# Inverting the mixer's triangular matrices on one side only, with 32x32 transposes on VectorE, in a hybrid RWKV-7 / gMLP / cross-attention / SwiGLU block

## The reference, cut to what matters

```
def step(S, inp):                 # one token, all heads
    r_t, w_t, k_t, v_t, kk_t, a_t = inp
    sa = jnp.einsum('bhvk,bhk->bhv', S, -kk_t)
    S = (S * w_t[:, :, None, :]
         + sa[..., None] * (kk_t * a_t)[:, :, None, :]
         + v_t[..., None] * k_t[:, :, None, :])
    y = jnp.einsum('bhvk,bhk->bhv', S, r_t)
    return S, y
```

## Time and profile before

| | |
|---|---|
| median of 3 runs | 3065.03 us (3062.26 to 3070.91) |
| span of the profiled execution, first to last instruction | 3061.7 us |
| PE, busy | 2955.4 us, 97% |
| DVE, busy | 1613.3 us, 53% |
| POOL, busy | 1432.3 us, 47% |
| ACT, busy | 1001.8 us, 33% |

### The profile page before, as it was taken

The page is one execution under the profiler, slowest core; times in us unless marked ns, Lnnn a source line. Parts: engine busy times, 40 slices in busy tenths (PEclk is TensorE's granted clock), DMA queues, the critical chain, the costliest instruction groups (busy, mean ns, idle before and its releaser), DMA issues.

```text
span 3061.7 us, 62501 instructions
## 1 busy us (share of the span) xinstructions
PE 2955.4 (97%) x26858; PEld 2523.8 (82%) x26858; DVE 1613.3 (53%) x2010; ACT 1001.8 (33%) x1692; POOL 1432.3 (47%) x993
## 2 busy tenths in 40 slices
PE   8999999989998989999999999999999999999998
PEld 7888888788888878998788888787898788888887
DVE  6332643365666653234866664545232876665452
ACT  4123211233443442233433332222232433332222
POOL 4555454333443445437544442446625654443344
PEclk9999999988998999999999999999999999999999
DMA  4433454321112222111223326454111123335642
GB/s 167 165 102 111 159 161 157 123 59 43 43 49 67 68 60 93 42 42 42 110 110 138 138 111 254 173 198 158 42 48 49 69 110 125 138 125 217 231 152 85
DMA packets 176012, 347.25 MB, mean 113 GB/s; under 512 B 47232, under 2 KB 104576, under 8 KB 170112
## 3 DMA queue, kind: packets, MB, share of 16 engines
q1 hardware_dynamic: 175744, 343.35, 32.5%
HBM read 240.53 MB, written 102.76 MB: 112 GB/s over the span
## 4 chain that ended last, share of the span: by engine, by line
PE 70%; DVE 6%; issue 2%; DMA 2%; ACT 1%; POOL 1%; SPq 0%; DVEq 0%; ACTq 0%; POOLq 0%
PE ps L2201 28%; PE ps L1641 19%; PE ps L2153 6%; PE ps L1747 2%; PE ps L1911 2%; PE ps L1913 2%; PE ps L1895 2%; PE ps L1865 1%; DMA w_raw<-in_weights 1%; DVE tu L2481 1%; DMA hidden<-hid 1%; PE ps L1992 1%; PE ps L1796 1%; PE ps L1819 1%; PE ps L1851 1%
## 5 line engine op out<-in xcount | busy, mean ns | idle before, releaser
L803 POOL TENSOR_TENSOR w_lo<-w_raw,w_hi 128x512 fp32r<-128x512 f32 x256 | 383.1, 1519 | 503.8 <-ACT w_hi L1093 500.0
L1641 PE MATMUL ps<-a_hi,w_hi 128*128 128x512 f32 x1140 | 446.3, 391 | 16.1 <-DVE a_lo L2381 9.6
L1641 PE MATMUL ps<-a_lo,w_hi 128*128 128x512 f32 x1140 | 444.4, 390 | 0.0
L1093 ACT ACTIVATE w_hi<-w_raw 128x512 fp32r<-128x512 f32 x252 | 144.8, 623 | 656.9 <-PE ps L1641 509.8
L1641 PE MATMUL ps<-a_hi,w_lo 128*128 128x512 f32 x1140 | 351.5, 390 | 0.0
L2201 PE MATMUL ps<-a_hi,w_hi 128*128 128x512 f32 x800 | 314.8, 393 | 10.3 <-ACT u_t L1462 4.9
L2201 PE MATMUL ps<-a_lo,w_hi 128*128 128x512 f32 x800 | 313.2, 391 | 0.0
L2201 PE MATMUL ps<-a_hi,w_lo 128*128 128x512 f32 x800 | 312.9, 391 | 0.0
L1641 PEld LDWEIGHTS ps<-a_hi,w_hi 128*128 128x128 f32 x1140 | 214.5, 188 | 62.9 <-DVE a_lo L2381 9.6
L1641 PEld LDWEIGHTS ps<-a_hi,w_lo 128*128 128x128 f32 x1140 | 214.3, 188 | 44.9
L1641 PEld LDWEIGHTS ps<-a_lo,w_hi 128*128 128x128 f32 x1140 | 214.5, 188 | 44.1 <-issue 0.2
(11 more groups left out here) (369 smaller groups left out, 6658.3 us busy)
## 6 DMA issues: line engine op xcount, KB each, us to landing
w_raw<-in_weights SPq DMA_DIRECT2D x228, 512.0 KB, 4.0
hidden<-hid SPq DMA_DIRECT2D x44, 1024.0 KB, 3.9
zT<-z_out SPq DMA_DIRECT2D x44, 512.0 KB, 3.8
a_hi<-hidden SPq DMA_DIRECT2D x44, 512.0 KB, 8.2
a_lo<-hidden SPq DMA_DIRECT2D x44, 512.0 KB, 9.1
w_raw<-kvw SPq DMA_DIRECT2D x32, 512.0 KB, 3.2
suv<-zT SPq DMA_DIRECT2D x16, 512.0 KB, 5.0
x<-in_xT SPq DMA_DIRECT2D x16, 512.0 KB, 6.1
```

The source lines that it names most:

```text
L803: pool.tensor_tensor(low_t[:, u, part, :], w_raw[:, u, part, :], high[:, u, part, :].bitcast(F32), ALU.subtract).then_inc(S["w_lo_done"], 1)
L1093: act.activation(split_into(pair)[0][:, u, part, :], w_raw[:, u, part, :], ACT.Copy).then_inc(S["w_hi_done"], 1)
L1641: mm = pe.matmul(to[:, nb, 0:w], wt[:, u, k, :], r[:, k, nb * w:(nb + 1) * w], start=(k == 0 and r is hi_in and wt is w_hi), stop=(k == kn ...
```

## The change

T is no longer computed on PE. The tile `tu`, which held T and U, becomes `inv`, which holds U alone, and `inv_t`, which holds T. DVE makes `inv_t` from `inv` by its 32x32 block transpose, two instructions a level (`turned`). The entries beside the diagonal are now copied with a mask straight from the scores in PSUM, so `first_pairs` and its semaphore are gone. T, U, `xm` and the right-hand sides all lie on the chunk's own lane a, so `up` is gone. Last, `body` is written in another order on PE and DVE; on ACT the order stays, and only `identities` gets half as long; on POOL nothing changes.

```diff
-            def up(e, a):
-                return a ^ 1 ^ e
+        def new_bank(lv, g):
+            return 2 * g + 1 if lv else 1 - g
...
             def cross(n, par, lv):
                 b = LEVELS[lv]
+                if lv == 0:
+                    pe.wait_ge(S["ev_b"], 2 * n + 2)
                 for g in range(2):
-                    pe.wait_ge(S["tu_ev"], 12 * n + 2 * lv + (g + 1 if lv else 2))
-                    for mh, e, a, h in by_tile(g):
-                        t_u = tu[par][lane(a), g, 0, e, mh, :].rearrange("p (n two b) -> p n two b", two=2, b=b)[:, :, 0, :]
-                        mm = pe.matmul(unit(h, 2 * g * (lv > 0) + e, 2 * L + g * C * (lv == 0) + mh * 32, 32),
-                                       atrb[par][lane(a), e, 2 * mh + g, 0, :], t_u, start=True, stop=True)
+                    if lv == 1 and g:
+                        pe.wait_ge(S["ev_k"], 2 * n + 2)
+                    pe.wait_ge(S["inv_tr"], 10 * n + 2 * lv + g + 1)
+                    for mh, e, a in by_tile():
+                        t_u = inv_t[lane(a), g, 2 * e + mh, :].rearrange("p (n two b) -> p n two b", two=2, b=b)[:, :, 0, :]
+                        mm = pe.matmul(unit(a, 2 * g * (lv > 0) + e, 2 * L + g * C * (lv == 0) + mh * 32, 32), atrb[par][lane(a), e, 2 * mh + g, 0, :], t_u,
+                                       start=True, stop=True)
                     mm.then_inc(S["x_ps"], 1)
...
             def merge(n, par, lv):
...
-                        if not last:
-                            t_at = (2 * g + 1, mh * 32) if e else (2 * g, BANK - C + mh * 32)
-                            pe.matmul(unit(a, *t_at, 32), u_u,
-                                      x_u.rearrange("p (n two b) -> p n two b", two=2, b=b)[:, :, 0, :], start=True, stop=True)
-                        mm = pe.matmul(unit(h, 2 * g + 1, (e + 1) * C + mh * 32, 32), x_u,
-                                       u_u.rearrange("p (n two b) -> p n two b", two=2, b=b)[:, :, 1, :], start=True, stop=True)
+                        mm = pe.matmul(unit(a, new_bank(lv, g), (e + 1) * C + mh * 32, 32), xm[lane(a), e, g, mh, :], u_u, start=True, stop=True)
...
             def from_values(k, par):
-                        mm = pe.matmul(unit(up(e, a), 4 + e, j * L + (m % 2) * C), qkrm[par][lane(a), e, m, 0, :], v_tok[par][lane(a), m, e, :],
+                        mm = pe.matmul(unit(a, 4 + e, j * L + (m % 2) * C), qkrm[par][lane(a), e, m, 0, :], v_tok[par][lane(a), m, e, :],
...
             def solve(k, par, j, last=False):
-                    mm = pe.matmul(unit(a, 6 + e, (2 + j) * L + (m % 2) * C), tu[par][lane(up(e, a)), m % 2, 1, e, m // 2, :],
-                                   rhs_t[lane(up(e, a)), e, m % 2, :], start=False, stop=True, skip_group_check=True)
+                    mm = pe.matmul(unit(a, 6 + e, (2 + j) * L + (m % 2) * C), inv[par][lane(a), e, m, :],
+                                   rhs_t[lane(a), e, m % 2, :], start=False, stop=True, skip_group_check=True)
...
+            def turned(n, par, lv):
+                for g in range(2):
+                    dve.wait_ge(S["tu_ev"], 11 * n + (2 * lv + g if lv else 1))
+                    dve.transpose(inv_t[:, g], units(inv[par], g)).then_inc(S["inv_tr"], 1)
...
             def take_level(n, par, lv):
                 b = LEVELS[lv]
                 for g in range(2):
                     dve.wait_ge(S["tu_ps"], 10 * n + 2 * lv + g + 1)
...
+                    take(rights(inv[par], g, b), low[:, lv + 1, 1].rearrange("p (m n b) -> p m n b", m=HP, b=b),
+                         ps[:, new_bank(lv, g), C:3 * C].rearrange("p (m n b) -> p m n b", m=HP, b=b), "tu_ev")
+                if lv + 1 < len(LEVELS):
+                    turned(n, par, lv + 1)
```

More of the change, by code:

```diff
@@ L238, in hybrid_block_kernel @@
         qkrm = [rw(f"qkrm{i}", [P, 2, HP, 2, C]) for i in range(2)]
-        tu = [rw(f"tu{i}", [P, 2, 2, 2, 2, C]) for i in range(2)]
+        inv = [rw(f"inv{i}", [P, 2, HP, C]) for i in range(2)]
+        inv_t = rw("inv_t", [P, 2, HP, C])
         gate = [tile4(f"gate{i}") for i in range(2)]
@@ L1867, in scores, with by_tile @@
                 mm.then_inc(S[done], 1)
[L1869 to L1886, removed]
+            def by_tile():
+                return [(mh, e, a) for mh in range(2) for e in range(2) for a in range(2)]
@@ L1901, in merge @@
                 b = LEVELS[lv]
[L1902 removed]
                 for g in range(2):
                     pe.wait_ge(S["x_ev"], 10 * n + 2 * lv + g + 1)
[L1905 to L1908, removed]
[L1909 to L1914 removed]
+                    for mh, e, a in by_tile():
+                        u_u = inv[par][lane(a), e, 2 * mh + g, :].rearrange("p (n two b) -> p n two b", two=2, b=b)[:, :, 1, :]
+                        mm = pe.matmul(unit(a, new_bank(lv, g), (e + 1) * C + mh * 32, 32), xm[lane(a), e, g, mh, :], u_u, start=True, stop=True)
                     mm.then_inc(S["tu_ps"], 1)
@@ L1958, in state_in @@
                 for m, e, a in by_pair(j):
[L1959 removed]
+                    mm = pe.matmul(unit(a, 4 + e, j * L + (m % 2) * C), qr[par][lane(e), 0, m, a, :], h_st[lane(e), j, m, :],
                                    start=False, stop=True, skip_group_check=True)
@@ L2009, in body @@
                     state_add(k, par, 0)
+                if behind:
+                    cross(b, q, 0)
+                if state:
                     chunk_out(k, par, 0)
-                if behind:
-                    first_pairs(b, q)
-                if state:
                     state_out(k, par, 1)
@@ L2016, in body @@
                 if behind:
-                    cross(b, q, 0)
+                    merge(b, q, 0)
                 if state:
@@ L2020, in body @@
                 if behind:
-                    merge(b, q, 0)
+                    cross(b, q, 1)
                 if state:
@@ L2024, in body @@
                 if behind:
-                    cross(b, q, 1)
+                    merge(b, q, 1)
                 if state:
@@ L2030, in body @@
                 if behind:
-                    merge(b, q, 1)
+                    cross(b, q, 2)
                 if ahead:
@@ L2035, in body @@
                     variance(k)
+                if behind:
+                    merge(b, q, 2)
                 if ahead:
@@ L2038, in body @@
                 if behind:
-                    cross(b, q, 2)
                     turn(b, kt, "kt_done", 4, ahead, "ktr")
-                    merge(b, q, 2)
+                    cross(b, q, 3)
                     turn(b, bt, "bt_done", 5, ahead, "btr")
-                    cross(b, q, 3)
+                    merge(b, q, 3)
                     turn_v(b, q, ahead, state)
-                    merge(b, q, 3)
+                    cross(b, q, 4)
                     bonus_sums(b, q)
@@ L2048, in body @@
                     key_scales(n)
+                if behind:
+                    merge(b, q, 4)
                 if state:
@@ L2488, in take_scores @@
                     take(dst[:, e].rearrange("p m w t -> p (m w t)"), triangles, ps[:, bank + e, :], done)
-            def blocks(ap, b):
-                return ap.rearrange("p u (n b) -> p u n b", b=b)
+            def turned(n, par, lv):
+                for g in range(2):
+                    dve.wait_ge(S["tu_ev"], 11 * n + (2 * lv + g if lv else 1))
+                    dve.transpose(inv_t[:, g], units(inv[par], g)).then_inc(S["inv_tr"], 1)
             def take_first(n, par):
-                dve.wait_ge(S["sc_1"], n + 1)
+                dve.wait_ge(S["sc_b"], n + 1)
                 dve.wait_ge(S["id_done"], n + 1)
[L2496 to L2500, removed]
+                odd_cols = inv[par][:].rearrange("p e m (x two) -> p e m x two", two=2)[:, :, :, :, 1]
+                mask = low[:, 0, 1].rearrange("p (m x) -> p m x", m=HP).unsqueeze(1).to_broadcast([P, 2, HP, C // 2])
+                take(odd_cols, mask, ps[:, 0:2, :].rearrange("p e (m w x two) -> p e m w x two", w=2, x=C // 2, two=2)[:, :, :, 0, :, 1], "tu_ev")
+                turned(n, par, 0)
             def take_level(n, par, lv):
@@ L2652, in body @@
                     keys_normed(n, state)
+                if scores:
+                    take_level(b, q, 4)
                 if state:
@@ L2657, in body @@
                     mixed(n)
-                if scores:
-                    take_level(b, q, 4)
-                if ahead:
                     decayed(n)
```

40 lines of the change are left out of this document (18 added, 22 removed).

## The result

The changed kernel takes 3101.49 us (median of 4 runs, 3089.15 to 3103.31) against 3064.24 us of the kernel before on the same chip (3062.26 to 3070.91): 1.0096 of it, 95% interval 1.0063 to 1.0129. It is slower, where 3049 us was forecast, and lies outside the range of 3029 to 3082 us. The profiled execution was its fastest, 3089.15 us at a mean clock of 0.977; the other three had 0.969 to 0.970. The ratios in this document leave out two slow runs, one of 3679.58 us at a mean clock of 0.746 in experiment 9 and one of 3074.43 us at 0.976 in experiment 6.

The account below looks back on a forecast made before the run. Took PE to bound the second part, code and DVE waits to slow the first. First part -1.5, second +1.0 us, times 16 = -8; clock -8; 3061.7 - 16 = 3045.7, plus 3.3: 3049 us; range 3029 to 3082 us.

Parts of the forecast that it names:

- the clock: Mixer bodies: the lower clock costs about 21 us before the change; 8 us of it credited as gain.
- the waits for code: First part of a body, PE's "issue" stretches: from 3.1 to 1.0 us, -2.1 us a body.
- Rival 2: The clock falls in the second part instead, 7 us at 1.2 GHz in two bodies of three, 21 us: 3064 us; chance 0.19.
- the end of the second part: After `merge` 4, half the scales (0.55) and 2.1 us for `lora_g` and `mix_gate`: ends at L + 18.3, L being the start of `loras`.
- terms for the second part at full clock: PE waits of 1.7 us at `merge` 3, 0.6 at `cross` 4, 0.3 at `merge` 4; the part +1.0 us.
- The transposes: DVE's block transposes, a price without a row: 0.37 us net each, about six of ten on the path.
- rival 3: The transpose on DVE is dear, 0.8 us each, adding 41 us: 3090 us; chance 0.10.
- A `cross` on two quarters: PE, each `cross` on two quarters of the array: from 0.60 to 1.0 us.
- The first part: Body from `from_values` to `loras`: from 14.5 us in the mean to 13.0 us, -1.5 us a body.
- `cross` 0 waits: First part, PE at `cross` 0: a new wait of 0.75 us for DVE's copies of the scores.
- rival 4: First part's code waits stay 3.1 us because they follow the transfers, +34 us: 3083 us; chance 0.13.
- Rival 1: Code waits vanish and the clock stays full, 1.9 us a body less: about 3034 us; chance 0.15.

Follow-up runs that it names:

- experiment 9: Kernel before, with only the turn of `bt` done as four plain matmuls instead of four transposes: 3069.83 us, 0.9998 of before.
- experiment 6: The change with its new order only up to `state_add` of the second half, old order behind it: 3042.51 us, 0.9920 of before.
- experiment 3: The change with `bt` turned by eight plain matmuls instead of four transposes, ahead of the wait at `merge` 3: 3051.32 us, 0.9948 of before.
- 8: The change with `scale_back` ahead of `merge` 4, third `xm` ahead of ACT's roots, level 3 ahead of DVE's reciprocals: 3025.02 us, 0.9844 of before.
- 5: The change's inverse in the old order, with `bt` turned by four plain matmuls instead of four transposes: 3025.90 us, 0.9851 of the kernel before.
- 10: 8 with the turn of `bt` done as four plain matmuls instead of four transposes: 3024.34 us, 0.9853 of the kernel before.

## Why the prediction was wrong

**Step that failed, the larger: the clock.** The sum credits 8 of the 21 us that the low clock was taken to cost before, because the waits for code shrink. They did shrink: the rows in which PE waits for "issue" between 645 and 1100 us add up to 31.5 us before and 9.9 after, 1.6 us a body less where 2.1 was forecast. But the fall moved to the second part and became dearer: 37 to 43 us (experiment 3). The term should have been 37 - 21 = +16 to 43 - 21 = +22 us instead of -8. The 21 us stay the prediction's estimate, since no run took the low clock away from the kernel before. Rival 2 named this mechanism and place, and priced it at 21 us. Its two bodies of three came true: 10 of the 15 second parts had a mean clock of 0.71 to 0.85 and took 21.4 to 24.8 us instead of 19.3. Its 7 us at half clock did not: that is what three of the ten show (0.84 to 0.85), while in the other seven (0.71 to 0.73) the half clock lasted 11 to 14 us, as in the rows of 771 to 785.5 us, from the wait at `merge` 3 to the end of the part. Before, the piece behind which it fell had PE busy for 1.44 us of 3.2; here one with 2.01 us is followed by a fall.

The Trainium skill, TensorE: Matmul & The Clock Gate, § HAM oscillation, gives two remedies for a matmul loop that waits for DMA: another loop order, so that TensorE stays busy, or padding the thin dimension of the matrix. Here the waits are for other engines, but the first agrees with the runs: mending the order gave 76 us (8). The second has only a likeness to experiment 3, in which matmuls that the result does not need gave 50 us; no run here padded a matrix.

**Step that failed, the smaller: the end of the second part.** "With that merge, half of the scales (0.55) and 2.1 for `lora_g` and `mix_gate` the part ends at L + 18.3" lets `mix_gate` run as soon as PE comes to it. `scale_back` was moved past `merge` 4, and what hangs on it (`kk`, level 4 and `y_n` in DVE's one queue) was not followed. The part measured 19.3 us at full clock, +1.0 us a body, 16 us, of which the wait is 0.86 us. The prediction's terms for the second part at full clock are otherwise right: waits of 1.18 and 0.81 us where it had 1.7 and 0.6, and none at `merge` 4 where it had 0.3.

**The sum again.** At full clock a body was to go from 31.8 to 31.3 us; it is 32.6 (experiment 3): +1.3, of which 1.0 is the missed wait and 0.2 to 0.5 the first part (13.2 to 13.55 us for 13.0). The low clock and what else the filling gives back add 2.7 - 1.36 = 1.34 us a body where -0.5 was credited: +1.8. (1.3 + 1.8) x 16 = 50 us, and 3049 + 50 = 3099 us. That this is near the median of 3101.5 us is luck: the rows come from the run of 3089.15 us, and for it the sum is 10 us too high. 7 of them are the shorter rest behind the last `identities`, which the prediction had at nothing and whose cause is open; the other runs of the change had a lower mean clock (0.970 against 0.977).

**What held.** The transposes, the disputed price: two in 0.76 to 0.77 us, 0.38 net against 0.37; rival 3 is out. The Trainium skill, Vector Engine (DVE) Microarchitecture Reference, § 3.8, led to an estimate of 0.27 us; the median of 421 ns is nearer to the copy than to it. A `cross` on two quarters takes 1.05 us (1.0 forecast). By the rule of the Trainium skill, TensorEngine Tiling (Array Packing), § Tiling Modes, the estimate was 1.2 us; the trace lies below it. The first part went from 14.5 us, the prediction's value at full clock, to 13.55 us: 0.95 us where 1.5 was forecast. In the mean of all bodies it shrank by 2.0 us (15.6 to 13.55), but there the clock, which no longer falls in it, has its share. `cross` 0 waits 1.08 us for the scores (0.75). Of the waits for code less than a third is left, so rival 4 is out. The prediction reckons them by four blocks of code where its rows show three transfers; that they are waits for code at all is its reading, which no run tried. Rival 1, a full clock at 3034 us, didn't come: at full clock the change's own order takes 3051 us (experiment 3), and 16 of the 17 us between them are the missed wait. Experiments 5, 8 and 10 get below it, in other orders.

**Open.** That the idle time of PE in the second part brings the clock down is shown by filling it and by removing it (3 and 8, with 9 as control; 5 points the same way). Why it falls in some bodies of one run and not in others with the same waits isn't. Of the five second parts of the change that kept their clock, three stand behind a longer first part, 14.4 to 14.9 us, but two behind one of 12.7 and 13.6 us. The cost of the transposes on the path was read from the trace, not tried by adding more.

## What to carry to other kernels

Where a step is moved in one engine's order, follow what it feeds around the other engines until it comes back: of the three waits that decided this case two came from ACT's and DVE's queues, which had not been moved along, or only in part, and one from a moved step of PE on whose signal DVE waited. And price a wait on TensorE by what it can do to the clock, not by its length: three waits of 2.85 us together went with a low clock that cost another 2.3 us a body or more. Where a wait can't be removed, a harmless matmul or two ahead of it is a cheap test and may be the mend.

## What the hardware showed unexpectedly

- Behind a wait of 1.19 us the granted clock fell to 0.50 and stayed near it for 13 us in which PE was busy throughout. With 1.4 us more matmuls ahead of that wait it was 1.00 over 455 us. Without them the same wait passed with the clock at 1.00 in the body at 869 us.
- The times of one kernel on one chip went with the mean clock: from 3028.3 us at 0.991 to 3063.0 us at 0.980 in experiment 6, 3.2 us per 0.001.
- Matmuls of 64x64 on 64x32 in float32 take 0.60 us per 16 on four quarters of the array and 1.05 us on two, less than double. A float32 transpose of 128x256 in blocks of 32 costs DVE as much as a copy, 0.42 us.
